# Inverse norms with tokens on partitions in the first mixer's preparation

## What is computed

```python
u, v, q, c_kv, q_idx, k_idx, w_idx, gates = split(proj)
y_a = chunked_spatial_gating(u, v, ...)            # gelu, layer norm of v, z = w_s @ v + b_s, u * z
c_n = rms_norm(c_kv, kv_norm_g)                    # 256 features
k   = rms_norm(c_n @ w_uk, k_norm_g)               # 128 features
vv  = c_n @ w_uv
qh  = rms_norm(q.reshape(4 heads, 128), q_norm_g)  # 128 features a head
qh, k   = partial_rope(qh), partial_rope(k)        # 32 rotated features
qi, ki  = partial_rope(q_idx), partial_rope(k_idx) # 16 rotated features
wi = w_idx * 4 ** -0.5
# rms_norm(x, g) = x * rsqrt(mean(x * x, over features) + 1e-6) * g
```

## Time and profile before

| | |
|---|---|
| median of 3 runs | 3269.1 us (3268.27 to 3269.39) |
| time of the profiled execution | 3270.03 us |
| its span, first to last instruction | 3268.0 us |
| PE busy | 2983.4 us, 91% |
| DVE busy | 1804.2 us, 55% |
| ACT busy | 1029.6 us, 32% |
| POOL busy | 844.8 us, 26% |
| mean granted PE clock | 0.945 |

### The profile page before, as it was taken

One profiled execution on the slowest core, in us unless ns is written; L12 is line 12 of the kernel. 1 busy time (PEld: TensorE's weight loads), 2 busy tenths in 40 slices (PEclk: granted clock), 3 DMA queues, 4 the chain that ended last, 5 costly groups with the idle time before them and its releaser, 6 DMA issues. The chain is left out here.

```text
span 3268.0 us, 41012 instructions
## 1 busy us (share of the span) xinstructions
PE 2983.4 (91%) x14322; PEld 2521.2 (77%) x14322; DVE 1804.2 (55%) x3734; ACT 1029.6 (32%) x1475; POOL 844.8 (26%) x511
## 2 busy tenths in 40 slices
PE   7669779999989999989999998999886998889997
PEld 6438668788868888879999996888765776768885
DVE  5566336756767775038888875443341445554423
ACT  3212313233234444223333333222211333132221
POOL 0013200344523333457666620000022212100000
PEclk9869889999989999989999999999986998899998
DMA  4003222344425555469999972333230212023331
GB/s 142 18 32 116 102 80 83 127 135 135 142 100 183 183 187 189 145 227 375 366 351 355 352 271 91 97 97 97 86 135 26 75 46 94 20 97 97 96 98 63
DMA packets 179308, 466.71 MB, mean 143 GB/s; under 512 B 21729, under 2 KB 71521, under 8 KB 177634
## 3 DMA queue, kind: packets, MB, share of 16 engines
q1 hardware_dynamic: 155490, 372.56, 34.3%
q0 software_dynamic: 22528, 67.19, 5.4%
q10 hardware_dynamic: 1152, 25.17, 1.8%
HBM read 395.44 MB, written 69.21 MB: 142 GB/s over the span
## 5 line engine op out<-in xcount | busy, mean ns | idle before, releaser
L54 PE MATMUL cb_y<-cb_g_hi,cb_b_hi 128*128 128x384 f32 x1024 | 343.2, 335 | 15.0 <-DVE cb_b_lo L1743 15.0
L55 PE MATMUL cb_y<-cb_g_lo,cb_b_hi 128*128 128x384 f32 x1024 | 342.9, 335 | 0.0
L56 PE MATMUL cb_y<-cb_g_hi,cb_b_lo 128*128 128x384 f32 x1024 | 342.8, 335 | 0.0
L186 DVE TENSOR_TENSOR ffn_lo<-ffn_raw,ffn_hi 128x1024 fp32r<-128x1024 f32 x132 | 161.4, 1226 | 273.6 <-ACT ffn_hi L182 273.5
L54 PE MATMUL ffn_bank<-x_hi,ffn_hi 128*128 128x512 f32 x704 | 277.7, 394 | 25.2 <-DVE x_lo L122 23.1
L55 PE MATMUL ffn_bank<-x_lo,ffn_hi 128*128 128x512 f32 x704 | 275.7, 392 | 0.0
L56 PE MATMUL ffn_bank<-x_hi,ffn_lo 128*128 128x512 f32 x704 | 275.4, 391 | 0.0
L491 POOL TENSOR_TENSOR bs_lo<-bs_raw,bs_hi 128x1024 fp32r<-128x1024 f32 x72 | 174.8, 2429 | 320.4 <-ACT bs_hi L468 320.4
L54 PE MATMUL bs_ps<-x_hi,bs_hi 128*128 128x512 f32 x576 | 232.3, 403 | 14.8 <-POOL bs_lo L491 14.8
L182 ACT CAST ffn_hi<-ffn_raw 128x1024 fp32r<-128x1024 f32 x132 | 138.0, 1048 | 301.4 <-PE ffn_bank L56 260.0
L1722 ACT CAST cb_b_hi<-cb_b_raw 128x1024 fp32r<-128x1024 f32 x128 | 134.6, 1052 | 297.8 <-PE cb_y L56 264.6
(11 more groups left out here) (461 smaller groups left out, 6666.7 us busy)
## 6 DMA issues: line engine op xcount, KB each, us to landing
cb_b_raw<-in_peer_v SPq DMA_DIRECT2D x128, 512.0 KB
ffn_raw<-in_gu SPq DMA_DIRECT2D x88, 512.0 KB, 3.6
bs_raw<-in_peer_u SPq DMA_DIRECT2D x72, 512.0 KB, 3.6
rs_raw<-in_peer_u SPq DMA_DIRECT2D x56, 512.0 KB, 3.6
routing<-br_out ACTq DMA_DIRECT2D x8, 3072.0 KB, 9.0
cb_route<-routing SPq DMA_DIRECT2D x32, 768.0 KB
cb_unit<-hidden SPq DMA_DIRECT2D x128, 192.0 KB
ffn_raw<-in_down SPq DMA_DIRECT2D x44, 512.0 KB, 3.6
```

Source lines behind the costliest of these rows:

```text
L54: pe.matmul(out, w_high, x_high, start=first, stop=False)
L55: pe.matmul(out, w_high, x_low, start=False, stop=False)
L56: return pe.matmul(out, w_low, x_high, start=False, stop=last)
L186: dve.tensor_tensor(lo[:, k % R, :], raw[:, k % R, :], hi[:, k % R, :].bitcast(F32), ALU.subtract).then_inc(split, 1)
```

## The change

The squares become the stationary operand and one column of ones the moving one. So each sum has its token on a partition, and one norm of 512 tokens is 4 columns (one for each tile of 128 tokens), 24 columns for the six norms. The c and q sums (20 columns) are taken together, scaled, rooted and inverted in one narrow operation each; those of k (4 columns) later. To apply them, PE spreads them back: one column of `rstd`, repeated 128 times as the stationary operand, times the identity gives a 128x128 tile whose rows all hold the 128 inverse norms; four make a bank (`spread`). DVE multiplies with this bank in place of `rstd`.

The order changes as well: on PE both sums stand first, the spreads lie between turns, k and vv, and the spread of k stands behind the gating products. On DVE the scalings of q are moved ahead of the layer norm of v, and so are the copies of k and vv and the mean square of k; the scaling of k is moved behind the gating.

```diff
-        ms = c.sb("m1_ms", [P, 2, SEQ])
-        rstd = c.sb("m1_rstd", [P, SEQ])
+        N_SUMS = TILES * (2 + N_HEADS)
+        ms = c.sb("m1_ms", [P, N_SUMS])
+        rstd = c.sb("m1_rstd", [P, N_SUMS])
-        JOBS = (["sum_c", "rot_qi0", "rot_qi1", "rot_ki"] + [f"sum_q{h}" for h in range(N_HEADS)]
-                + ["k", "vv", "sum_k"] + [f"z{g}" for g in range(A_GROUPS)]
+        JOBS = (["sum_c", "sum_q", "rot_qi0", "rot_qi1", "rstd_c", "rot_ki", "rstd_q0", "rstd_q1", "k", "rstd_q2", "vv",
+                 "rstd_q3", "sum_k"] + [f"z{g}" for g in range(A_GROUPS)] + ["rstd_k"]
                 + [f"rot_q{h}" for h in range(N_HEADS)] + ["rot_k", "wi"])
+        SUMS_OF = {"c": 0, **{f"q{h}": TILES * (1 + h) for h in range(N_HEADS)}, "k": TILES * (1 + N_HEADS)}
...
-                for n in range(1 + N_HEADS):
-                    root(n)
+                act.wait_ge(S["ms"], 2)
+                act.activation(ms[:, :SUMS_OF["k"]], ms[:, :SUMS_OF["k"]], ACT.Sqrt).then_inc(S["root"], 1)
...
-                def mean_square(x, features, n):
+                def mean_square(x, at, count, features):
                     take(x)
-                    dve.tensor_scalar(ms[:, n % 2, :], bank(x)[:], 1.0 / features, EPS, ALU.mult, ALU.add
+                    dve.tensor_scalar(ms[:, at:at + count], bank(x)[:, :count], 1.0 / features, EPS, ALU.mult, ALU.add
                                       ).then_inc(S["ms"], 1)
...
+                def normed(x, tile, gain):
+
+                    take(f"rstd_{x}")
+                    dve.scalar_tensor_tensor(tile, tile, gain, bank(f"rstd_{x}")[:], ALU.mult, ALU.mult
+                                             ).then_inc(S["normed"], 1)
+                    done_norms[0] += 1
+                    dve.wait_ge(S["normed"], done_norms[0])
+                    dve.sem_inc(took, 1)
...
+                mean_square("sum_c", SUMS_OF["c"], TILES, KV_LATENT)
+                mean_square("sum_q", SUMS_OF["q0"], TILES * N_HEADS, P)
                 for kind in (R128, R64):
                     ...
+                dve.wait_ge(S["root"], 1)
+                dve.reciprocal(rstd[:, :SUMS_OF["k"]], ms[:, :SUMS_OF["k"]]).then_inc(S["rstd"], 1)
                 rope("rot_qi0", proj[:, QI0, :], R64)
                 rope("rot_qi1", proj[:, QI0 + 1, :], R64)
+                take("rstd_c")
+                (two multiplications of the c tiles with gains and bank("rstd_c"))
                 rope("rot_ki", proj[:, KI0, :], R64)
+                normed("q0", proj[:, Q0, :], gains[:, 2:3])
+                normed("q1", proj[:, Q0 + 1, :], gains[:, 2:3])
+                take("k"), copy to kT
+                normed("q2", proj[:, Q0 + 2, :], gains[:, 2:3])
+                take("vv"), copy to vv
+                normed("q3", proj[:, Q0 + 3, :], gains[:, 2:3])
+                mean_square("sum_k", SUMS_OF["k"], TILES, P)
                 (layer norm of v)
+                dve.wait_ge(S["root"], 2)
+                dve.reciprocal(rstd[:, SUMS_OF["k"]:], ms[:, SUMS_OF["k"]:]).then_inc(S["rstd"], 1)
                 (gating z0 to z3)
+                normed("k", kT[:], gains[:, 3:4])
...
+                def sums(x, squares, at):
+
+                    for t in range(TILES):
+                        for i, n in enumerate(squares):
+                            last = pe.matmul(bank(x)[:, at + t:at + t + 1], sq[:, n, t * P:(t + 1) * P], ones[:, 0:1],
+                                             start=i == 0, stop=i == len(squares) - 1)
+                    return last
+
+                def spread(x):
+
+                    start(f"rstd_{x}")
+                    for t in range(TILES):
+                        at = SUMS_OF[x] + t
+                        last = pe.matmul(bank(f"rstd_{x}")[:, t * P:(t + 1) * P],
+                                         rstd[:, at:at + 1].broadcast_to([P, P]), ident[:], start=True, stop=True)
+                    finish(last)
```

More of the change, by code:

```diff
@@ L826, in gate_and_prepare @@
             "small", "positions", "const", "masked", "gelu", "vt", "ln_var", "ln_sd", "vnorm", "seq",
-            "sq", "job", "took", "ms", "root", "half", "angle", "sines", "normed", "gated", "low")}
+            "sq", "job", "took", "ms", "root", "rstd", "half", "angle", "sines", "normed", "gated", "low")}
         small, job, took, seq = S["small"], S["job"], S["took"], S["seq"]
@@ L892, in _ @@
                 act.activation(sd[:], sd[:], ACT.Sqrt).then_inc(S["ln_sd"], 1)
-                for n in range(1 + N_HEADS):
-                    root(n)
+                act.wait_ge(S["ms"], 2)
+                act.activation(ms[:, :SUMS_OF["k"]], ms[:, :SUMS_OF["k"]], ACT.Sqrt).then_inc(S["root"], 1)
                 act.wait_ge(took, NUM["k"] + 1)
                 act.activation(sq[:, 2 + N_HEADS, :], kT[:], ACT.Square).then_inc(S["sq"], 1)
-                root(1 + N_HEADS)
+                act.wait_ge(S["ms"], 3)
+                act.activation(ms[:, SUMS_OF["k"]:], ms[:, SUMS_OF["k"]:], ACT.Sqrt).then_inc(S["root"], 1)
                 for g in range(A_GROUPS):
@@ L938, in _ @@
                     dve.tensor_scalar(sd[:], mv[:, :, 1], EPS, None, ALU.add).then_inc(S["ln_var"], 1)
-                def mean_square(x, features, n):
+                def mean_square(x, at, count, features):
                     take(x)
-                    dve.tensor_scalar(ms[:, n % 2, :], bank(x)[:], 1.0 / features, EPS, ALU.mult, ALU.add
+                    dve.tensor_scalar(ms[:, at:at + count], bank(x)[:, :count], 1.0 / features, EPS, ALU.mult, ALU.add
                                       ).then_inc(S["ms"], 1)
-                    dve.wait_ge(S["ms"], n + 1)
+                    dve.wait_ge(S["ms"], {"sum_c": 1, "sum_q": 2, "sum_k": 3}[x])
                     dve.sem_inc(took, 1)
-                def reciprocal_root(n):
-                    dve.wait_ge(S["root"], n + 1)
-                    then(dve.reciprocal(rstd[:], ms[:, n % 2, :]))
+                def normed(x, tile, gain):
[5 more added lines that the diff above has]
+                    dve.sem_inc(took, 1)
+                done_norms = [0]
                 def rope(x, tile, kind):
@@ L971, in _ @@
                     then(dve.tensor_scalar(cos[kind][:], cos[kind][:], -2.0, 1.0, ALU.mult, ALU.add))
+                dve.wait_ge(S["root"], 1)
+                dve.reciprocal(rstd[:, :SUMS_OF["k"]], ms[:, :SUMS_OF["k"]]).then_inc(S["rstd"], 1)
                 rope("rot_qi0", proj[:, QI0, :], R64)
                 rope("rot_qi1", proj[:, QI0 + 1, :], R64)
-                rope("rot_ki", proj[:, KI0, :], R64)
+                take("rstd_c")
+                for k in range(2):
+                    last = dve.scalar_tensor_tensor(proj[:, C0 + k, :], proj[:, C0 + k, :], gains[:, k:k + 1],
+                                                    bank("rstd_c")[:], ALU.mult, ALU.mult)
+                last.then_inc(S["normed"], 1)
+                done_norms[0] += 1
+                dve.wait_ge(S["normed"], done_norms[0])
+                dve.sem_inc(took, 1)
+                rope("rot_ki", proj[:, KI0, :], R64)
+                normed("q0", proj[:, Q0, :], gains[:, 2:3])
+                normed("q1", proj[:, Q0 + 1, :], gains[:, 2:3])
+                take("k")
+                dve.tensor_copy(kT[:], bank("k")[:]).then_inc(took, 1)
+                normed("q2", proj[:, Q0 + 2, :], gains[:, 2:3])
+                take("vv")
+                dve.tensor_copy(vv[:].rearrange("p t n -> p (t n)"), bank("vv")[:]).then_inc(took, 1)
+                normed("q3", proj[:, Q0 + 3, :], gains[:, 2:3])
+                mean_square("sum_k", SUMS_OF["k"], TILES, P)
                 dve.wait_ge(S["ln_sd"], 1)
@@ L1026, in _, with turn @@
                 pe.wait_ge(small, 16 * len(SMALL))
+                def sums(x, squares, at):
[11 more added lines that the diff above has]
+                    finish(last)
+                def turn(x, kind, tile):
+                    start(x)
+                    finish(pe.matmul(bank(x)[:], rot[:, kind, :], tile, start=True, stop=True))
                 start("sum_c")
                 pe.wait_ge(S["sq"], 2)
-                for k in range(2):
-                    last = pe.matmul(bank("sum_c")[:], ones[:], sq[:, k, :], start=k == 0, stop=k == 1)
-                finish(last)
[L1032 to L1039, removed]
+                finish(sums("sum_c", (0, 1), 0))
+                start("sum_q")
+                pe.wait_ge(S["sq"], 2 + N_HEADS)
+                for h in range(N_HEADS):
+                    last = sums("sum_q", (2 + h,), TILES * h)
+                finish(last)
+                turn("rot_qi0", R64, proj[:, QI0, :])
+                turn("rot_qi1", R64, proj[:, QI0 + 1, :])
+                pe.wait_ge(S["rstd"], 1)
+                spread("c")
+                turn("rot_ki", R64, proj[:, KI0, :])
+                spread("q0")
+                spread("q1")
                 pe.wait_ge(S["normed"], 1)
@@ L1044, in _ @@
                 finish(last)
```

(9 more changed lines are left out.)

3 lines of the change are left out of this document (removed).

## The result

| | before | after |
|---|---|---|
| median | 3267.9 us (3266.51 to 3269.39, 6 runs) | 3244.14 us (3242.62 to 3248.05, 6 runs) |
| time and span of the profiled execution | 3270.03, 3268.0 us | 3247.84, 3246.1 us |

The ratio is 0.9929 with a 95% interval of 0.9917 to 0.9942: 23 us faster, between 19 and 27.

What follows compares the result with a forecast made beforehand. In the first mixer's preparation, DVE's reciprocals and waits were taken as the bound, with PE's gating products standing behind them. Gating 22.3 us sooner, tail 1.2 longer: -21.1 us, median 3248.0 us, range 3243 to 3257.

Steps and rivals of the forecast that it cites:

- The reciprocals carry it: On DVE, first mixer's preparation: six 128x512 reciprocals, 20.1 us, are removed; two short ones of 0.18 and 0.28 us are added.
- The price of a column sum at half clock: On PE, column sums of c and q: 0.217 us a pass, barely dependent on the number of moving columns.
- its clock: On PE, column sums of c and q: half clock for all 48 passes, 10.6 us, sums ready at 139.9.
- The rule on weight loads: PE's column sums: load priced by weight columns, one moving column saves nothing; its 107 ns would give 5.1 us, not 10.4.
- PE's clock behind the sums: On PE, turns and spreads following the sums without a gap: full clock from about 144.5 until PE waits for c.
- rival A: PE stays at half clock behind the sums and sets the pace: gating at 171.5, saving 14.6 us, 3254.5; chance 0.18.
- its second form: Column sums at 0.36 us a pass, spreads as forecast: sums at 146.7, saving 14.3 us, 3254.8; chance 0.08.
- Gating and tail: Stage's end: gating products unchanged at half clock, 22.99 us; tail 14.9 us instead of 13.71, 1.2 us longer.
- B: Column sums on PE nearly free, reciprocal done at 139.1 instead of 142.8: saving 24.8 us, 3244.3; chance 0.12.
- C: Sums and spreads at 0.36 us and PE at half clock: gating at 185.2, +0.3 us, 3269.4, no change; chance 0.05.
- D: Short products and repeated-column spread weights load at 0.433 us a pass on a cold PE: +7.7 us, 3276.8; chance 0.02.
- E: The stage's saving is hidden from the kernel's time or not made; chance 0.02.

Runs made afterwards that it cites:

- the order: The kernel before with DVE's layer norm of v moved behind the copies of k and vv, nothing else: 3266.14 us, ratio 0.9991.
- the first of these runs: The kernel before with its six reciprocals cut to 4 columns and scalings multiplying with the root itself, inverse left out: 3252.95 us, ratio 0.995.
- four of its variants: The changed kernel with k's spread early (3244.68 us, one execution), four turns out of the tail (3239.91), one bias product per gating group (3236.97), everything together (3227.34).
- the doubled sums: The changed kernel with the column sums of c and q made twice over, 96 passes instead of 48: 3258.11 us, ratio 0.9967.
- the second set of runs: The changed kernel run once more, nothing edited: 3246.95 us (3243.09 to 3249.63), ratio 0.9928.
- the early spread: The changed kernel with k's inverse, spread and scaling made ahead of the gating products: 3244.68 us, one execution, only its trace used.

## Why the prediction came out as it did

**The reciprocals carry it: right.** Their length alone, 15.86 us ahead of the gating where 15.9 were worked out. With 1.94 for the order, 7.5 of the 25.3 us are left for the rest. The rows account for them: five mean squares of 0.68 against three of under 0.2 us (2.9), the waits for ACT's root, 2.65 and four of 0.70, which nothing replaces (5.4), and 0.4 for the short reciprocals, five of 0.18 us in the first of these runs against 0.28 and 0.17 now. Against them stand 0.85 us of new wait for the sums and some 0.8 for the waits of 0.15 us at PE's banks, which leaves 7.1 of the 7.5. This last split is arithmetic from the traces; no run took the waits out alone.

**The price of a column sum at half clock: right; its clock: the step that was off.** The forecast had all 48 passes at 0.217 us, 10.6 us in all, and the sums ready 14.8 us after the angles' start (139.9 - 125.07). The first trace has 7.66 us and 11.8: passes came 0.114 us apart from 130.0 to 133.2, (133.2 - 130.0)/28, at a clock of 0.97, and at half clock behind that. Ahead of them stand the transposes of v, 3.64 of 3.70 us busy at 0.50, and the clock was up when the sums began. I had read the clock off other short passes and did not ask what PE does just before these. The 3.0 us are the whole of the gating's lead over the forecast (25.3 against 22.3). They are luck in part. Six traces have these 48 passes behind the same transposes, two of the changed kernel and four of its variants. All six began them at full clock and lost it on the way; the sums took 7.66 to 9.32 us and were ready 11.8, 13.6, 12.5, 13.6, 14.2 and 12.7 us after the angles (also because PE began them 4.1 to 4.8 us after the angles). So the forecast was too late each time, by 0.6 to 3.0 us, and the first trace is the far end. In the trace of before and in that of the doubled sums the passes behind the same transposes began at half clock.

The times show the same. The median here is 3.9 us below the forecast, that of the second set of runs 1.1 (3246.95). The traced span, 3246.1, stands near the forecast's 3246.9 by luck: the stage gave 2.9 us more than forecast, and 2.1 of its gain did not reach the end of the kernel.

**The rule on weight loads** (the Trainium skill, "TensorE: Matmul & The Clock Gate", section "LDWEIGHTS (loading the stationary operand)"): the Trainium skill prices a load by the columns of the weights alone. The trace agrees that one moving column saves nothing: 0.114 us for one column against 0.115 for 31 and 0.122 for 128, at full clock. The estimate of 107 ns that follows from the Trainium skill's figure is near this at full clock only; at half clock the passes here took 0.214 us, and the measurement decides.

**PE's clock behind the sums: right.** 0.50 until 143.2, 1.00 from 144 to 153 (forecast: from 144.5). So rival A, PE setting the pace at half clock, did not come, nor did its second form, sums at 0.36 us a pass, and DVE met the spreads, k and vv with waits of about 0.15 us each. The ordering of the steps held: c scaled at 144.86 (forecast 147.2 with the later sums), mean square of k at 153.36 (156.0).

**Gating and tail: right.** 23.12 us at clock 0.50 for 22.99 forecast; tail 14.87 for 14.9, of which the moved spread of k is what the early spread gave back (13.69).

**B came in time, not in mechanism.** It forecast 3244.3 us, and the median is 3244.14. In the first trace the sums held DVE up for only 0.85 us of the forecast's 3.7, which is near B; in the second for 2.60. But they are not nearly free: a second set of them put gating back by 11.6 us and more. What hid most of them was the clock.

**C and D fell.** The spreads, with their one repeated column, cost 0.11 us a pass at full clock ((1.95 - 0.275)/15 = 0.112) like any others; the zero step in the weights cost nothing here. **E fell in the main**: the stage's saving is the kernel's, but not to the last. The stage is 24.0 us shorter, the next stage's ACT begins 23.2 sooner (its first instruction on `sel_relu` at 204.5 instead of 227.7), the first gate output 22.4 sooner (225.0, 247.4), the merge's first product 21.8 sooner (356.3, 378.1), and the span 21.9. The first 0.8 us of this loss stood ahead of the stage, which began that much later in this trace. The 0.8 us between 23.2 and 22.4 is PE's clock. The gate products after the change, then before:

```profile
221.34 0.59 PE L55 MATMUL gs_ps<-x_lo,gs_hi 128*128 128x512 f32 x1
221.76 0.39 PE L56 MATMUL gs_ps<-x_hi,gs_lo 128*128 128x512 f32 x1
...
242.79 0.60 PE L54 MATMUL gs_ps<-x_hi,gs_hi 128*128 128x512 f32 x1
243.22 0.40 PE L55 MATMUL gs_ps<-x_lo,gs_hi 128*128 128x512 f32 x1
```

The gate stream starts at 216.91 and reaches the short duration at 221.76, after 4.85 us at clock 0.50; before, it started at 240.07 and had it at 243.22, after 3.15. The 1.7 us more at half the clock cost about 0.85 us. Whether such gains and losses at other restarts of PE add up to the spread between runs, 5 us for six runs, was not shown; I did not trace it through the other stages.

## What to carry to other kernels

A reciprocal or a root for each token is best made where tokens lie on partitions: 512 values along the free axis cost DVE 3.35 us for the reciprocal, the same 512 in 4 columns 0.18 us (ACT's root 0.63 us, and 0.20 even for 20 columns), and a product with the identity spreads them back for eight short passes. Price the new PE work by its weight loads and by the clock that PE has when it gets there. Look at what stands just ahead of it, and give a range: behind the same transposes the sums began at full clock in six traces, and twice over at half clock in another. When the chain has been moved off one engine, look at what now runs alone: here the gating products, 23 of 75 us, whose alternating weights and idle neighbours gave another 16 us of the stage (74.91 to 59.10).

## What the runs showed of the hardware that was not expected

- 96 passes with one moving column kept PE busy for 20.4 of 20.4 us, and the granted clock was 0.50 (1.2 GHz) throughout. In the trace of the changed kernel, PE was busy with the same passes for 3.20 of 3.20 us at 0.97 and for 3.80 of 3.80 us behind that at 0.50.
- At 1.2 GHz, 128-column passes alternating between weights of 128 rows and of 1 row were 0.36 us apart, and 0.237 us among their own kind; each change of kind cost about 0.3 us.
- Column sums of the same kernel took 7.66 or 8.85 us in two executions, with PE never idle in them: 3.1 or 1.7 us of them ran at full clock.
- A DVE multiplication of two SBUF operands, 0.69 us alone, took 1.59 us where POOL's low part ran from just before it; it ended 0.55 us behind POOL.
